# A two-pass fp32r gate product in an attention and expert-lookup block on one Trainium2 core

## The reference, cut to what matters

```python
s1, i1 = lax.top_k(s[:, :, 0], PEER_TOPK)            # 16 best of 128 first keys, per head (8 heads)
s2, i2 = lax.top_k(s[:, :, 1], PEER_TOPK)            # 16 best of 128 second keys
cand = s1[..., :, None] + s2[..., None, :]           # 256 sums, of which the 16 best are kept
idx = i1 * N_KEYS + i2                               # expert number, one of 128 * 128
g = softmax(top_s)                                   # one weight per chosen expert
h = gelu(einsum('ted,td->te', u[idx], x));  out = einsum('te,ted->td', g * h, v[idx])
```

## Time and profile before

| | us |
|---|---|
| median of 3 runs | 3251.55 (3249.18 to 3255.22) |
| the profiled execution | 3252.24 |
| its span | 3250.5 |
| TensorE busy | 3216.1 (99%) |
| VectorE busy | 2263.4 (70%) |
| ScalarE busy | 1119.1 (34%) |
| GpSimd busy | 933.6 (29%) |

### The profile page before, as it was taken

How to read it: one execution, slowest core, us unless ns; L and a number is a source line. 1 busy time by engine, 2 the same in 40 slices (tenths; PEclk the granted TensorE clock), 3 DMA queues, 4 the chain that set the end, 5 groups by cost and what they waited for, 6 DMA issues and landing times. The chain is left out here.

```text
span 3250.5 us, 41510 instructions
## 1 busy us (share of the span) xinstructions
PE 3216.1 (99%) x16730; PEld 2818.6 (87%) x16730; DVE 2263.4 (70%) x2636; ACT 1119.1 (34%) x1172; POOL 933.6 (29%) x424
## 2 busy tenths in 40 slices
PE   8999999999999999999999999999999999999999
PEld 6878778887878899999999899889989988888887
DVE  5666541113027888887874888888889888888887
ACT  5232323334232233655553223223222322222221
POOL 4333333333434321111101323223322321223222
PEclk9999999999999999999999999999999999999999
DMA  3222222223233247889877989999989998888888
GB/s 144 78 78 90 77 78 78 78 78 141 92 116 121 88 161 255 304 316 318 311 243 265 352 333 352 336 341 345 358 332 335 350 343 312 320 336 340 343 319 317
DMA packets 171364, 777.87 MB, mean 239 GB/s; under 512 B 14064, under 2 KB 80752, under 8 KB 86384
## 3 DMA queue, kind: packets, MB, share of 16 engines
q1 hardware_dynamic: 127488, 457.77, 38.6%
q0 software_dynamic: 43776, 318.79, 26.3%
HBM read 731.10 MB, written 44.34 MB: 239 GB/s over the span
## 5 line engine op out<-in xcount | busy, mean ns | idle before, releaser
L419 PE MATMUL bank<-xh,wh 128*128 128x336 f32 (+1 forms) x3184 | 1105.8, 347 | 1.6 <-DVE wl L1128 1.6
L421 PE MATMUL bank<-xh,wl 128*128 128x336 f32 (+1 forms) x3184 | 1090.1, 342 | 0.0
L420 PE MATMUL bank<-xl,wh 128*128 128x336 f32 (+1 forms) x3184 | 1088.2, 342 | 0.0
L399 ACT ACTIVATE wh<-raw 128x2048 fp32r<-128x2048 f32 x344 | 658.0, 1913 | 999.0 <-PE bank L446 723.3
L1128 DVE TENSOR_TENSOR wl<-raw,wh 128x2048 fp32r<-128x2048 f32 x252 | 576.8, 2289 | 215.2 <-ACT wh L399 214.9
L419 PEld LDWEIGHTS bank<-xh,wh 128*128 128x128 f32 x3184 | 599.3, 188 | 46.5 <-issue 3.8
L420 PEld LDWEIGHTS bank<-xl,wh 128*128 128x128 f32 x3184 | 599.5, 188 | 44.7 <-issue 1.9
L421 PEld LDWEIGHTS bank<-xh,wl 128*128 128x128 f32 x3184 | 598.2, 188 | 45.1
L405 POOL TENSOR_TENSOR wl<-raw,wh 128x2048 fp32r<-128x2048 f32 x92 | 424.9, 4618 | 739.5 <-ACT wh L399 739.5
L444 PE MATMUL bank<-wh,xh 128*128 128x512 f32 x1072 | 417.1, 389 | 0.8 <-DVE stat L1302 0.8
L446 PE MATMUL bank<-wh,xl 128*128 128x512 f32 x1072 | 417.0, 389 | 0.0
(11 more groups left out here) (211 smaller groups left out, 2803.3 us busy)
## 6 DMA issues: line engine op xcount, KB each, us to landing
raw<-in_u SPq DMA_DIRECT2D x128, 1024.0 KB, 5.8
raw<-in_v SPq DMA_DIRECT2D x128, 1024.0 KB, 6.2
raw<-in_w_in SPq DMA_DIRECT2D x56, 1024.0 KB, 4.8
gate_scratch<-arena SPq DMA_DIRECT2D x12, 2048.0 KB
arena<-gate_scratch SPq DMA_DIRECT2D x32, 768.0 KB, 9.0
raw<-in_w_out SPq DMA_DIRECT2D x16, 1024.0 KB, 4.9
raw<-in_w_pq SPq DMA_DIRECT2D x16, 1024.0 KB, 4.9
act_scratch<-arena SPq DMA_DIRECT2D x68, 168.0 KB, 4.4
```

Of the source, the lines that this page charges most:

```text
L399: nc.scalar.activation(wh[s][:], raw[s][:], ACT.Copy).then_inc(hi_done, 1)
L419: nc.tensor.matmul(dst, w_h[:, c], xh[:, c, 0:width], start=(c == 0), stop=False)
L420: nc.tensor.matmul(dst, w_h[:, c], xl[:, c, 0:width], start=False, stop=False)
L421: last = nc.tensor.matmul(dst, w_l[:, c], xh[:, c, 0:width], start=False, stop=(c == KC - 1))
```

## The change

Both operands of the gate product become fp32r, and the product is done in two passes that are summed in the bank. The weight rows are held as a high part (`hot_hi`, the weight rounded to fp32r, times the one-hot row) and a second part (`hot_lo`). VectorE now writes `hot_hi` for all 96 batches. ScalarE writes `hot_lo` for all 96: for each token one copy of the high rows, scaled per slot by rest/high, so that it gives the rest of the weight where the high row is not zero. These ratios are computed once per 128 tokens by seven small VectorE instructions (`weight_rest`), after `take_slots`, and once more for 48 tokens. The eight-instruction form on ScalarE (`Abs`, `Relu`) and its helper `minus_g` go. Both row sets have two buffers each, in `gl` and in a third of `gh`. In iteration k ScalarE does `rows_act` of the first batch of unit k+1 before it copies out the two batches of unit k-1, and of the second batch after. TensorE waits on `row_done`, ScalarE's count, for every batch.

```diff
-ACT_ROWS = [_b for _b in range(0, (TD - PT - PB) // 4, 2 * GATE_STEP)]
+LARGE = 1.0e34
...
             def rows_act(b):
-                mine = slotT[b // 32 % 2]
-                act.wait_ge(minus_done, b // 32 + 1)
-                act.wait_ge(gate_done, b + 1)
-                for n in range(4 * (b % 32), 4 * (b % 32) + 4):
-                    dst = hot_gate[b % 2][:, n % 4 * P:n % 4 * P + P]
-                    nc.scalar.activation(dst, iota128[:], ACT.Abs, bias=mine[:, 0, n:n + 1],
-                                         scale=-1.0).then_inc(diff_step, 1)
...
+                act.wait_ge(hot_done, b + 1)
+                for n in range(4):
+                    piece = slice(n * P, n * P + P)
+                    token = 4 * (b % 32) + n
+                    last = nc.scalar.activation(hot_lo[b % 2][:, piece], hot_hi[b % 2][:, piece].bitcast(F32), ACT.Copy,
+                                                scale=rest_of[b // 32 % 2][:, token:token + 1])
                 last.then_inc(row_done, 1)
...
+                ahead = GATE_STEP * (k + 1 - GATE_FROM)
+                if 0 <= ahead < DB * 32:
+                    rows_act(ahead)
                 if GATE_FROM < k <= GATE_FROM + GATE_UNITS:
...
-                if GATE_STEP * (k + 1 - GATE_FROM) in ACT_ROWS:
-                    rows_act(GATE_STEP * (k + 1 - GATE_FROM))
+                if 0 <= ahead < DB * 32:
+                    rows_act(ahead + 1)
...
             def hot(b):
...
-                for n in range(n0, n0 + 4) if b not in ACT_ROWS else ():
-                    last = nc.vector.tensor_scalar(hot_gate[b % 2][:, (n - n0) * P:(n - n0 + 1) * P], iota128[:],
+                for n in range(n0, n0 + 4):
+                    last = nc.vector.tensor_scalar(hot_hi[b % 2][:, (n - n0) * P:(n - n0 + 1) * P], iota128[:],
                                                    turned_slots[:, 0, n:n + 1], turned_slots[:, 2, n:n + 1],
                                                    ALU.is_equal, ALU.mult)
...
+            def weight_rest(t, tokens=slice(0, P)):
+                w = slotT[t % 2][:, 2, tokens]
+                high, small, rest = (b[:, tokens] for b in rest_tmp)
+                rested(nc.vector.tensor_copy(high.bitcast(F32R), w))
+                nc.vector.tensor_tensor(rest, w, high, ALU.subtract)
+                rested(nc.vector.tensor_scalar(small, high, 0.0, None, ALU.is_equal))
+                rested(nc.vector.tensor_tensor(small, small, high, ALU.add))
+                rested(nc.vector.reciprocal(small, small))
+                rested(nc.vector.tensor_scalar(small, small, LARGE, -LARGE, ALU.min, ALU.max))
+                rested(nc.vector.tensor_tensor(rest_of[t % 2][:, tokens], rest, small, ALU.mult))
...
             def gate_batch(b, i):
-                pe.wait_ge(hot_done, i * (4 * GATE_STEP) + b + 1)
-                if b % 4 == 0:
-                    pe.wait_ge(row_done, i * GATE_STEP + b // 4 + 1)
+                pe.wait_ge(row_done, i * (4 * GATE_STEP) + b + 1)
                 pe.wait_ge(gate_out, i * (4 * GATE_STEP) + b + 1)
                 for n in range(4):
-                    mm = nc.tensor.matmul(GATE_BANKS[b % 4][:, n * P:(n + 1) * P],
-                                          gh[:, (b % 2) * 512 + n * P:(b % 2) * 512 + (n + 1) * P].bitcast(F32),
-                                          hot_gate[b % 2][:, n * P:(n + 1) * P], start=True, stop=True)
+                    nc.tensor.matmul(GATE_BANKS[b % 4][:, piece], keys, hot_hi[b % 2][:, piece], start=True, stop=False)
+                    mm = nc.tensor.matmul(GATE_BANKS[b % 4][:, piece], keys, hot_lo[b % 2][:, piece], start=False,
+                                          stop=True)
```

More of the change, by code:

```diff
@@ L242, in build @@
         pb_dots = at(12432 - NB, NB)
-        look = gl[:, 0:1024]
-        minus_g = at(7040, P)
+        look = at(8592, 1024)
+        rest_tmp = [at(8592 + P * n, P) for n in range(3)]
+        rest_of = [at(7040, P), ones[:]]
         gate_piece = at(0, NKEYS * GT)
         h_out = [at(9616 + D, UT), at(9616 + D + UT, UT)]
-        hot_gate = [at(8592, 512), at(8592 + 512, 512)]
+        hot_hi = [gl[:, 0:512], gl[:, 512:1024]]
+        hot_lo = [gl[:, 1024:1536], gh[:, 1024:1536]]
         rows_g = [at(0, D), at(D, D), at(4096 + 2 * GRP * TD, D)]
@@ L338, in build @@
         hot_done = sem("hot_done")
-        minus_done = sem("minus_done")
-        diff_step = sem("diff_step")
+        rest_step = sem("rest_step")
         row_done = sem("row_done")
@@ L1436, in lookup @@
                 picked(nc.vector.tensor_tensor(
-                    look4, look4.bitcast(F32),
+                    look4, look4,
                     idx_f[:, t, 4 * half:4 * half + 4, c, :].unsqueeze(2).broadcast_to([P, PH // 2, TOPK, TOPK]),
                     ALU.mult))
-                nc.vector.tensor_reduce(slots[t][:, c, 64 * half:64 * half + 64], look3.bitcast(F32), AX.X,
+                nc.vector.tensor_reduce(slots[t][:, c, 64 * half:64 * half + 64], look3, AX.X,
                                         ALU.add).then_inc(slots_done, 1)
@@ L1459, in hot, with rested @@
                     turned_slots[:, 1, n0:n0 + 4].unsqueeze(2).broadcast_to([P, 4, NKEYS]), ALU.is_equal)
[L1460 to L1467, removed]
-                for n in range(n0, n0 + 4) if b not in ACT_ROWS else ():
-                    last = nc.vector.tensor_scalar(hot_gate[b % 2][:, (n - n0) * P:(n - n0 + 1) * P], iota128[:],
+                for n in range(n0, n0 + 4):
+                    last = nc.vector.tensor_scalar(hot_hi[b % 2][:, (n - n0) * P:(n - n0 + 1) * P], iota128[:],
                                                    turned_slots[:, 0, n:n + 1], turned_slots[:, 2, n:n + 1],
                                                    ALU.is_equal, ALU.mult)
-                    if b % 4 == 0 and n == n0:
-                        last.then_inc(row_done, 1)
                 last.then_inc(hot_done, 1)
+            rests = [0]
+            def rested(ins):
+                rests[0] += 1
+                ins.then_inc(rest_step, 1)
+                dve.wait_ge(rest_step, rests[0])
+            def weight_rest(t, tokens=slice(0, P)):
[8 more added lines that the diff above has]
+                rested(nc.vector.tensor_tensor(rest_of[t % 2][:, tokens], rest, small, ALU.mult))
             dve.wait_ge(lo_done, LO_DVE)
@@ L1540, in _ @@
                     take_slots(0)
+                    weight_rest(0)
                 for j, at_unit in enumerate(DOT_UNITS):
@@ L1566, in _ @@
                         take_slots(t)
+                        weight_rest(t)
                 if k == PAIR_TURN:
                     take_pair()
+                    weight_rest(DB - 1, slice(P - PT - PB, P))
                 if k == LOOK_AT[DB] + 4:
@@ L1963, in gate_batch @@
             def gate_batch(b, i):
-                pe.wait_ge(hot_done, i * (4 * GATE_STEP) + b + 1)
-                if b % 4 == 0:
-                    pe.wait_ge(row_done, i * GATE_STEP + b // 4 + 1)
+                pe.wait_ge(row_done, i * (4 * GATE_STEP) + b + 1)
                 pe.wait_ge(gate_out, i * (4 * GATE_STEP) + b + 1)
                 for n in range(4):
-                    mm = nc.tensor.matmul(GATE_BANKS[b % 4][:, n * P:(n + 1) * P],
-                                          gh[:, (b % 2) * 512 + n * P:(b % 2) * 512 + (n + 1) * P].bitcast(F32),
-                                          hot_gate[b % 2][:, n * P:(n + 1) * P], start=True, stop=True)
+                    piece = slice(n * P, (n + 1) * P)
+                    keys = gh[:, (b % 2) * 512 + n * P:(b % 2) * 512 + (n + 1) * P]
+                    nc.tensor.matmul(GATE_BANKS[b % 4][:, piece], keys, hot_hi[b % 2][:, piece], start=True, stop=False)
+                    mm = nc.tensor.matmul(GATE_BANKS[b % 4][:, piece], keys, hot_lo[b % 2][:, piece], start=False,
+                                          stop=True)
                 mm.then_inc(gate_done, 1)
```

## The result

The changed kernel takes 3376.8 us (median of 5 runs, 3376.2 to 3379.4), the kernel before 3252.7 (5 runs, 3249.2 to 3258.2). The ratio is 1.0383, 95% interval 1.0369 to 1.0397: 124 us slower. The forecast was 3382 in a range of 3350 to 3430.

What follows compares the result with a forecast made beforehand. The prediction took TensorE to set the pace before, and a closed ring of ScalarE and VectorE after. 3252.2 + 113.3 (rounds, less the end) + 16 (store) = 3381.5, said as 3382 us, range 3350 to 3430.

Steps and rivals of the forecast that it cites:

- The ring: Gate stage: ScalarE and VectorE wait for each other within each round, so rounds cannot overlap; 10.46 to 13.50 us, above TensorE's 9.17.
- Every class of round: Rounds sorted by VectorE's work between its two hot calls: one pair_dot 11.29 us, two 13.50, a lookup 12.85, neither 10.46.
- the 47 rounds: Gate-stage iterations k = 16 to 62: forecast 558.6 us against 441.0 before, +117.6, less 4.3 at the end.
- a gather: Gathers that pair_dot waits for, 21.6 us of waits before: they get more time and no longer matter.
- it cost nothing, as forecast: weight_rest on VectorE, about 3 us three times and a shorter one: hidden while VectorE would wait for ScalarE anyway.
- The term for the store: ScalarE's eleven waits for the store of a gate piece lengthen rounds: +16 us, ends 0 and 35.
- the mean landing, 11.1 us: Store of a gate piece: time from its issue until ScalarE can go on, derived from eleven waits before the change.
- The prediction's lower bound: Store's low end: all stores land within 10 us at the lower traffic, cost 0, which is -16 us.
- The sum, 3381.5: Whole kernel: 3252.2 + 113.3 + 16 = 3381.5, said as 3382 us.
- TensorE's batches: Gate product on TensorE: a batch costs 0.56 to 0.9 us, taken as 0.87; no gain, as it is outside the ring.
- Where TensorE idles: Gate stage: TensorE idle about 100 us, most of it between units, waiting for VectorE's lo.
- the rival that this lengthens the stage: Gate stage: gaps lower TensorE's clock; at half clock for half of the units 154 us more, 3535; chance 4%.

Runs made afterwards that it cites:

- late_second_rows: Changed kernel with ScalarE's copies for the second batch of a unit made one round later, all work kept; 3254.2 us, ratio 1.0010 to the kernel before.
- no_wait_on_rows: Changed kernel with ScalarE's scaled copies reading a constant tile, so nearly all its waits for VectorE's rows go; 3247.9 us, ratio 0.9984 to the kernel before.
- one_pass: Changed kernel without the second matmul pass, four matmuls a batch instead of eight, ScalarE's second rows still made; 3375.6 us, ratio 1.0383 to the kernel before.
- rows_before_dots: Changed kernel with VectorE making both batches' rows directly after lo, lookups and dots behind them; 3316.6 us, ratio 1.0204 to the kernel before.
- before_rows_first: Kernel before the change, with ScalarE's rows of every fourth batch made before the two copies out of PSUM; 3244.2 us, ratio 0.9979.
- late_and_store_rounds: late_second_rows, plus in eleven store rounds the next unit's first-batch rows made before the copies out of PSUM; 3250.2 us, ratio 1.0002 to the kernel before.

## Why the prediction was right

**The ring.** Every class of round came out within 0.04 us of its sum, but one: one dot 11.25 (11.29 forecast), two dots 13.46 (13.50), lookup 12.81 (12.85), none 10.26 (10.46). The last is shorter since two copies out of PSUM take 1.7 us there instead of 1.86 (1843.38 to 1845.10). With these the 47 rounds sum to 8 x 12.81 + 21 x 11.25 + 10 x 13.46 + 8 x 10.26 = 555.4 us (558.6 forecast). late_second_rows and no_wait_on_rows show the cause from two sides, the order and the wait; one_pass and rows_before_dots show that TensorE is outside and the dots inside.

**What lies over the ring.** 568.5 - 555.4 = 13.1 us, where the prediction had 16, all of it for the store. The excess, round by round:

- 7.2 us in rounds with a store. ScalarE waited for it in five of eleven, 17.7 us in all. In two of these (29 and 41, one dot) the round grew by 3.2 and 2.9; in the three with two dots (21, 33 and 45) VectorE's longer round hid all but 1.1.
- 4.0 us in rounds 25, 37 and 49, each behind one with two dots: the dot waits for a gather (3.7 us), which the prediction put at nothing.
- 1.5 us for work of VectorE between the dots and `hot(a+1)` that the prediction left out: `pair_weights` in round 54 (1.1) and a memset in round 20 (0.4).
- 0.4 us in single rounds. `weight_rest` is in this: it took 2.6 us and made the round behind it 0.07 longer, so it cost nothing, as forecast.

The term for the store was too large since it gave the mean landing, 11.1 us, to every store. In the changed kernel six of the eleven landed 8.1 to 8.8 us after their issue, before ScalarE needed them, and the five others after 12.4 to 13.5. The longest wait (4.05 us) ends 13.5 us behind its issue, 1436.74 to 1450.23:

```profile
1436.74 0.39 SPq L663 DMA_DIRECT2D gate_scratch<-arena  x1
```

```profile
1450.23 1.02 ACT L1061 ACTIVATE arena<-bank 128x512 f32<-128x512 f32 x1 [4.05 <-DMA gate_scratch<-arena]
```

The prediction's lower bound had all stores land early, at the lower traffic of a slower stage. The runs do not show that traffic decides it: late_second_rows, at 283 GB/s, has three late landings (12.1 to 13.9 us) and a median of 8.5; the changed kernel, at 221, has five and a median of 9.0.

**The start.** 1.3 us, left out: the first rows wait for VectorE before round 16.

**What was luck.** The sum, 3381.5, lies 2.9 us over the profiled execution (3378.6), but not each term did so well. Rounds and store were 12 us too large; gathers, other work, start and the 1.8 us behind the stage (not traced to a cause) were 9 us too small.

**TensorE's batches.** Forecast 0.87 us and no gain. The weight loads of one batch of the changed kernel, with the next load of the big products:

```profile
1402.80 0.19 PEld L1981 LDWEIGHTS bank<-gl,gh 128*128 128x128 f32 x1 [0.57 <-ACT gh L1038]
1402.90 0.19 PEld L1982 LDWEIGHTS bank<-gh 128*128 128x128 f32 x1
...
1403.57 0.19 PEld L1982 LDWEIGHTS bank<-gh 128*128 128x128 f32 x1
1403.68 0.19 PEld L420 LDWEIGHTS bank<-xh,wh 128*128 128x128 f32 x1
```

Eight loads, (1403.57 - 1402.80) / 7 = 0.11 us apart, as for fp32 operands, and 0.88 us for the batch. In late_second_rows a unit takes 9.15 us instead of 9.17: this is all that two fp32r passes give over one fp32 product of this size. The 81 ns of the Trainium skill ("TensorE: Matmul & The Clock Gate", section "Back-to-back issue gap") are not reached with 4-byte weights here; the measurement decides.

**Where TensorE idles.** This part was wrong. I had most of its 100 idle us between units, for `lo`. The sum is right (101), but the waits show 53.8 us for the copies out of PSUM, 34.8 for `lo` and 11.9 for rows. In the changed order the bank copies stand behind `rows_act(a)` and so behind the first wait for VectorE; the batch that needs the bank comes first. As TensorE is not in the ring, this cost nothing.

**The clock.** TensorE did fall to half its clock (0.50 at 1352 to 1355, behind a wait of 3.7 us for the bank copies; mean 0.97 in the stage, 0.95 in one_pass), and the rival that this lengthens the stage fell: in one_pass the mean clock was lower still and the time the same.

## What to carry to other kernels

An engine with a third of its time free can still set the pace: ask not only how much it does but in which order, and follow each wait through both instruction lists until it comes back to where it began. If it does, add up the ring by starts, class of round by class of round; here that gave 129 us forecast for 124 measured. The repair is to consume a result one round later than it is made, which brought back 123 of the 124 us. And what another engine needs soon goes ahead of an instruction that waits for a store, if it does not wait for something else itself: that was worth 7 us in before_rows_first and left TensorE's waits nearly as they were in late_and_store_rounds.

## What the runs showed of the hardware

A matmul with 128 x 128 weights of 4 bytes and 128 columns costs 0.11 us whether it is half of an fp32 product or a pass in fp32r; only fewer of them made a batch cheaper (0.43 us for four). The runs halve weight loads and matmuls together, so they do not tell which of the two sets the 0.11. Writing fp32r instead of fp32 cost VectorE nothing (1.11 us for four rows of 128 columns both times), and ScalarE's scaled copies, which read fp32 and write fp32r, took 1.24 to 1.28 us for four, as its `Abs` of the same shape from fp32 to fp32 did.
